# Four of eighteen modulation parts computed by VectorE passes over the weight chunks instead of TensorE matmuls

## The reference, cut to what matters

```python
mx = jnp.split((jax.nn.silu(c) @ w_mod[l] + b_mod[l])[:, None, :], N_MOD, axis=-1)
mz = jnp.split(jax.nn.silu(c_ctx) @ w_mod[l] + b_mod[l], N_MOD, axis=-1)
x = x + 0.5 * mx[2] * swiglu(modulate(rms_norm(x), mx[0], mx[1]), ffn1_w1[l], ffn1_w3[l], ffn1_w2[l])
z = z + 0.5 * mz[2] * swiglu(modulate(rms_norm(z), mz[0], mz[1]), ffn1_w1[l], ffn1_w3[l], ffn1_w2[l])
hx = modulate(rms_norm(x), mx[3], mx[4]) @ w_in[l]
hz = modulate(rms_norm(z), mz[3], mz[4]) @ w_in[l]
...
```

## Time and profile before

| what | value |
|---|---|
| median of 3 runs | 3135.41 us (3133.4 to 3138.79) |
| the profiled execution, its own time | 3135.46 us |
| its span, first to last instruction | 3133.7 us |
| mean granted TensorE clock | 0.989 of 2.4 GHz |
| loads of `w_mod` | 72 of 1 MB |

### The profile page before, as it was taken

The page is one execution under the profiler, slowest core; times in us unless marked ns, Lnnn a source line. Parts: engine busy times, 40 slices in busy tenths (PEclk is TensorE's granted clock), DMA queues, the critical chain, the costliest instruction groups (busy, mean ns, idle before and its releaser), DMA issues.

```text
span 3133.7 us, 54005 instructions
## 1 busy us (share of the span) xinstructions
PE 3013.5 (96%) x23072; PEld 2751.5 (88%) x23072; DVE 1799.8 (57%) x2813; ACT 1480.5 (47%) x2222; POOL 151.3 (5%) x147
## 2 busy tenths in 40 slices
PE   6999999999999998999999989999999999999998
PEld 5899888898889998899898789999899989989997
DVE  4456555656556545455655555465856656486665
ACT  3344454453555443444454444456654445655443
POOL 0000000002000000000200000001010101111000
PEclk9999999999999999999999999999999999999999
DMA  7765445654555555765355445554355655435563
GB/s 276 276 221 167 161 138 199 208 188 144 157 201 174 181 189 202 259 216 168 118 186 169 152 158 188 188 176 129 111 166 190 199 186 163 126 107 170 166 200 133
DMA packets 409691, 556.65 MB, mean 178 GB/s; under 512 B 25277, under 2 KB 357997, under 8 KB 409069
## 3 DMA queue, kind: packets, MB, share of 16 engines
q1 hardware_dynamic: 409452, 553.20, 52.9%
HBM read 552.12 MB, written 1.05 MB: 177 GB/s over the span
## 4 chain that ended last, share of the span: by engine, by line
PE 83%; DVE 8%; DMA 3%; ACT 3%; issue 3%; SPq 0%; POOL 0%; DVEq 0%; ACTq 0%
PE psum L119 24%; PE psum L121 23%; PE psum L120 23%; PE psum L710 1%; DVE wl L276 1%; DMA wr<-in_ffn_w_dram 1%; DVE wl L2166 1%; PE psum L1906 1%; PE psum L2331 1%; PE psum L1528 1%; PE psum L2437 1%; PE psum L2415 1%; PE psum L1183 1%; PE psum L1515 1%; DMA wr<-in_w_mod_dram 1%
## 5 line engine op out<-in xcount | busy, mean ns | idle before, releaser
L276 DVE TENSOR_TENSOR wl<-wr,wh 128x1024 fp32r<-128x1024 f32 (+1 forms) x558 | 658.0, 1215 | 232.2 <-ACT wh L265 231.3
L265 ACT ACTIVATE wh<-wr 128x1024 fp32r<-128x1024 f32 (+1 forms) x558 | 554.5, 1039 | 249.2 <-DMA wr<-in_ffn_w_dram 228.3
L119 PE MATMUL psum<-xt_hi,wh 128*128 128x256 f32 (+1 forms) x2000 | 565.9, 283 | 3.7 <-DVE wl L276 2.4
L120 PE MATMUL psum<-xt_lo,wh 128*128 128x256 f32 (+1 forms) x2000 | 558.1, 279 | 0.0
L121 PE MATMUL psum<-xt_hi,wl 128*128 128x256 f32 (+1 forms) x2000 | 558.0, 279 | 0.0
L2166 DVE TENSOR_TENSOR wl<-wr,wh 128x1024 fp32r<-128x1024 f32 (+3 forms) x336 | 391.8, 1201 | 120.8 <-ACT wh L2158 119.5
L119 PEld LDWEIGHTS psum<-xt_hi,wh 128*128 128x128 f32 (+1 forms) x2000 | 377.3, 189 | 16.0 <-issue 8.1
L120 PEld LDWEIGHTS psum<-xt_lo,wh 128*128 128x128 f32 (+1 forms) x2000 | 376.8, 188 | 2.4
L121 PEld LDWEIGHTS psum<-xt_hi,wl 128*128 128x128 f32 (+1 forms) x2000 | 377.6, 189 | 0.1
L119 PE MATMUL psum<-wh,xt_hi 128*128 128x256 f32 (+1 forms) x1280 | 370.4, 289 | 2.4 <-ACT vv L3316 1.9
L2158 ACT ACTIVATE wh<-wr 128x1024 fp32r<-128x1024 f32 (+3 forms) x336 | 322.5, 997 | 100.8 <-DMA wr<-in_mlp_w_dram 72.2
(11 more groups left out here) (466 smaller groups left out, 5378.9 us busy)
## 6 DMA issues: line engine op xcount, KB each, us to landing
wr<-in_ffn_w_dram SPq DMA_DIRECT2D x231, 1024.0 KB, 5.2
wr<-in_w_in_dram SPq DMA_DIRECT2D x88, 1024.0 KB, 5.1
wr<-in_w_mod_dram SPq DMA_DIRECT2D x72, 1024.0 KB, 4.8
wr<-in_mlp_w_dram SPq DMA_DIRECT2D x64, 1024.0 KB, 5.2
wr<-in_w_out_dram SPq DMA_DIRECT2D x20, 1024.0 KB, 4.9
wr<-in_mem_w_kv_dram SPq DMA_DIRECT2D x8, 1024.0 KB, 4.9
wr<-in_w_branch_dram SPq DMA_DIRECT2D x16, 512.0 KB, 3.4
wr<-in_w_branch_dram SPq DMA_DIRECT2D x8, 1024.0 KB, 4.8
```

Source lines behind the costliest of these rows:

```text
L119: pe.matmul(out, a[0], b[0], start=first, stop=False)
L120: pe.matmul(out, a[0], b[1], start=False, stop=False)
L265: act.activation(self.high[s][:, r], self.raw[s][:, r], ACT.Copy).then_inc(self.highs.sem, 1)
L276: dve.tensor_tensor(self.low[s][:, r], self.raw[s][:, r], self.high[s][:, r].bitcast(F32), ALU.subtract).then_inc(self.lows.sem, 1)
```

## The change

Parts 3 and 4 of layer 0 and parts 4 and 5 of layer 1 (16 of 72 modulation pieces) become `ScaledPiece`s. For each of the 8 blocks of 128 rows of `w_mod` in a part VectorE multiplies the chunk's half [128 x 1024] by a column of one stream and adds it to an accumulator [128 x 1024] for that stream, and the same for the other: four passes for each piece. These passes (`ahead`) stand in VectorE's program in the piece before the scaled one, after its own subtraction steps and ahead of `lo_ahead`. TensorE does nothing in pieces i = 0, 1, 2; in piece 3 it does 16 matmuls with an accumulator block [128 x 128] as weights and one column of ones, which sum over the partitions, and VectorE copies and biases the 16 columns. Pieces 0 to 2 aren't counted as `used` by themselves: the next piece of TensorE waits for the accumulator and adds them to its own increment at its end (`w.use`). In `zf1`, `weave(..., 1, 2)` becomes `weave(..., 1, 3)`, so that its ten modulation pieces stand three pieces apart.

```diff
+    def use(self, last, own=1):
+        last.then_inc(self.used.sem, own + len(self.scaled_by))
+        self.scaled_by = []
...
     def split(self, pe, m):
+        self.scaled(pe)
         pe.wait_ge(self.lows.sem, 2 * self.pieces[m].parted_before + 2)
...
         if not self.over_raw(m + 1):
             self.lo(dve, m + 1, h)
+        if m + 1 < len(self.pieces):
+            self.pieces[m + 1].ahead(dve, h)
...
+class ScaledPiece(ModulationPiece):
+    def wait_scaled(self, eng):
+        mod = self.mod
+        eng.wait_ge(mod.acc.sem, mod.acc.at(2 * self.nth + 2))
+
+    def ahead(self, dve, h):
+        w, b, mod = self.w, self.mod.b, self.mod
+        s = self.m % RING
+        if h == 0:
+            dve.wait_ge(w.loaded[s].sem, w.loaded[s].at(self.m // RING + 1))
...
+        col = 2 * (2 * self.i + h)
+        chunk = w.raw[s][:, :].rearrange("p (k n) -> p k n", n=D)[:, h, :]
+        for v in range(2):
+            acc, scalar = b["acc"][mod.l][:, v, :], b["silu"][:, col + v:col + v + 1]
+            if self.i == 0 and h == 0:
+                last = dve.tensor_scalar(acc, chunk, scalar, None, ALU.mult)
+            else:
+                last = dve.scalar_tensor_tensor(out=acc, in0=chunk, scalar=scalar, in1=acc, op0=ALU.mult, op1=ALU.add)
+        last.then_inc(mod.acc.sem, 1)
+        dve.wait_ge(mod.acc.sem, mod.acc.at(2 * self.nth + h + 1))
+
+    def pe(self, pe, step):
...
+        w.scaled_by.append(self)
+        if self.i == 3:
+            w.scaled(pe)
+            b["ones_set"](pe)
+            bank = w.claim(pe, self.u0)
+            w.touch()
+            for k in range(KT):
+                for v in range(2):
+                    at = 2 * k + v
+                    last = pe.matmul(bank[:, at:at + 1], b["acc"][mod.l][:, v, k * P:(k + 1) * P], b["ones"][:, 0:1], start=True, stop=True)
+            w.use(last, 0)
...
+    def dve(self, dve, step):
...
+        if self.i == 3:
+            w.used_up(dve, self.m)
+            turned = b["turned"][:, 0, 0:2 * KT]
+            dve.tensor_copy(turned, w.ps[:, 6 + self.u0 % 2, 0:2 * KT]).then_inc(w.bank_free[self.u0 % 2].sem, 1)
+            w.emptied(dve, self.u0)
...
-    order += weave(zf1.pieces, M0[10:20], 1, 2)
+    order += weave(zf1.pieces, M0[10:20], 1, 3)
```

More of the change, by code:

```diff
@@ L292, in lo_ahead, with scaled @@
             self.lo(dve, m + 2, 1)
+    def scaled(self, pe):
+        for piece in self.scaled_by:
+            piece.wait_scaled(pe)
+    def use(self, last, own=1):
+        last.then_inc(self.used.sem, own + len(self.scaled_by))
+        self.scaled_by = []
     def split(self, pe, m):
+        self.scaled(pe)
         pe.wait_ge(self.lows.sem, 2 * self.pieces[m].parted_before + 2)
@@ L360, in sp @@
         self.w.load(sp, self.m + RING)
+    def ahead(self, dve, h):
+        pass
     def early(self, eng_name, eng):
@@ L601, in pe @@
                     last = split_product(pe, out[:, t, :], a, b, k == 0, k == self.nk - 1)
-            last.then_inc(w.used.sem if i == self.n_units - 1 else proj.part.sem, 1)
+            if i == self.n_units - 1:
+                w.use(last)
+            else:
+                last.then_inc(proj.part.sem, 1)
     def empty(self, eng, i):
@@ L656, in pe @@
             last = split_product(pe, bank[0:32, 0:256], [v[:, k, :] for v in wv], [v[:, k, :] for v in self.lhs], k == 0, k == KT - 1)
-        last.then_inc(w.used.sem, 1)
+        w.use(last)
     def late(self, name, eng):
@@ L670, in __init__ @@
         self.w, self.l, self.b = w, l, b
-        self.pieces = [ModulationPiece(self, part, i, chunk_of(w_mod, 2 * i * P, 2, part * D, D)) for part in range(9) for i in range(4)]
+        kind = lambda part: ScaledPiece if part in b["scaled"][l] else ModulationPiece
+        self.pieces = [kind(part)(self, part, i, chunk_of(w_mod, 2 * i * P, 2, part * D, D)) for part in range(9) for i in range(4)]
+        self.acc = None
         self.summed = w.share("mod_summed", 36)
@@ L742, in dve, with __init__, ahead @@
         ins.then_inc(mod.summed.sem, 1)
+        w.lo_ahead(dve, self.m)
+class ScaledPiece(ModulationPiece):
+    room = None
+    def __init__(self, mod, part, i, src):
+        super().__init__(mod, part, i, src)
+        self.n_units = 1 if i == 3 else 0
+        self.nth = 4 * sorted(mod.b["scaled"][mod.l]).index(part) + i
+    def wait_scaled(self, eng):
+        mod = self.mod
+        eng.wait_ge(mod.acc.sem, mod.acc.at(2 * self.nth + 2))
+    def ahead(self, dve, h):
+        w, b, mod = self.w, self.mod.b, self.mod
+        s = self.m % RING
+        if h == 0:
+            dve.wait_ge(w.loaded[s].sem, w.loaded[s].at(self.m // RING + 1))
+            if self.i == 0:
+                b["ready"](dve)
+                if self.room:
+                    self.room(dve)
+        col = 2 * (2 * self.i + h)
[4 more added lines that the diff above has]
+                last = dve.tensor_scalar(acc, chunk, scalar, None, ALU.mult)
+            else:
+                last = dve.scalar_tensor_tensor(out=acc, in0=chunk, scalar=scalar, in1=acc, op0=ALU.mult, op1=ALU.add)
+        last.then_inc(mod.acc.sem, 1)
+        dve.wait_ge(mod.acc.sem, mod.acc.at(2 * self.nth + h + 1))
+    def pe(self, pe, step):
+        w, b, mod = self.w, self.mod.b, self.mod
+        self.some(step, 0)
+        w.scaled_by.append(self)
[9 more added lines that the diff above has]
+            w.use(last, 0)
+        self.some(step, 1)
+    def dve(self, dve, step):
+        w, b, mod = self.w, self.mod.b, self.mod
+        w.lo_next(dve, self.m, 0)
+        w.lo_next(dve, self.m, 1)
+        self.some(step, 0)
+        self.some(step, 1)
+        if self.i == 3:
[3 more added lines that the diff above has]
+            w.emptied(dve, self.u0)
+            bias = b["bias"][:, mod.l, self.part * KT:(self.part + 1) * KT].unsqueeze(2).to_broadcast([P, KT, 2])
+            dve.scalar_tensor_tensor(out=b["mod"][mod.l][:, self.part * KT:(self.part + 1) * KT, :],
+                                     in0=turned.rearrange("p (k v) -> p k v", v=2), scalar=0.5 if self.part in (2, 8) else 1.0, in1=bias,
+                                     op0=ALU.add if self.part in (1, 4, 7) else ALU.mult, op1=ALU.add).then_inc(mod.summed.sem, 4)
@@ L3670, in first_block @@
     silu = at("silu_cond", [P, 48], F32, 187)
-    mod_b = dict(mod=c["mod"], silu=silu, turned=mod_turned, bias=c["bias"])
+    mod_ones = small("mod_ones", 1)
+    mod_b = dict(mod=c["mod"], silu=silu, turned=mod_turned, bias=c["bias"],
+                 acc=[at(f"mod_acc{l}", [P, 2, D], F32, (116, 132)[l]) for l in range(LAYERS)], ones=mod_ones, scaled={0: (3, 4), 1: (4, 5)}, ones_set=lambda eng: eng.wait_ge(zeroed.sem, zeroed.at(1)))
     turn_b = dict(tmp=at("affine", [P, 4, 256], F32, 108), diag=c["diag"], var=c["var"], root=c["root"], root_tmp=c["root_tmp"])
@@ L3879, in first_block @@
     urgent, background, order = [], [], []
+    for mod in mods:
+        n = 4 * len(mod_b["scaled"][mod.l])
+        mod.acc = w.share("cond_cleared", 2 * n)
     zf1, xf1 = ffn(0, 1, Z), ffn(0, 1, X)
@@ L3983, in first_block @@
     zf3.down[7].spread(mods[1], 5, X.v, rows2, x_out.wait_added)
+    mods[1].pieces[16].room = xm.turn.wait_done
     x_in1 = InProjection(w, A["w_in"][1], X.pair, X.h, gate_t(X, 1), x_t8.wait_done)
@@ L4107, in gpsimd @@
         w.pool_link = Chain(pool, w.pool_step)
+        pool.memset(mod_ones[:, :], 1.0)
         pool.memset(gw[:, :], 0.0).then_inc(zeroed.sem, 1)
```

## The result

The changed kernel takes 3152.46 us (median of 6 runs, 3147.47 to 3154.46), the kernel before 3134.88 (6 runs, 3132.28 to 3138.79): a ratio of 1.0051, 95% interval 1.0041 to 1.0061, so 17.6 us slower. The profiled execution took 3153.94 (span 3152.2, mean granted clock 0.987), 18.5 more than the one of before, 3135.46.

A forecast was written before the change was run, and what follows sets the result against it. The prediction took TensorE, busy 96% of the span, as the bound. It summed -16.0 + 13.6 + 10.4 + 5.1 = +13.1 onto 3135.4 us, forecasting 3148 us, with a range of 3132 to 3161.

The forecast's parts named there:

- What is taken away: On TensorE, 16 modulation pieces of 1.00 us each go: -16.0 us.
- The 16 one-column matmuls of piece 3: On TensorE, 16 matmuls in each of four parts, at 0.2125 us each, 3.4 us a part: +13.6 us.
- The floor for few columns: Skill page's floor of about 25 ns for 1 to 64 columns: 0.8 us a part, 3.2 in all; not adopted.
- that rival: In piece 3, one-column matmuls are cheap, 0.0625 us a record, +8.0 us: about 3139 us in all; chance 0.12.
- The late load: Next modulation chunk is requested only after the following TensorE piece; eight TensorE waits of 1.3 us: +10.4 us.
- Path 1: On VectorE, late chunk's landing, four passes and the subtraction end at 17.89 us, against a deadline of 16.67.
- path 2: The following piece's own load queues behind the late chunk; its subtraction ends at 17.95 us, against a deadline of 16.67.
- queued loads don't slow the first: On SP's queue, a load requested shortly behind another leaves the first's landing time at 4.8 us.
- The clock: TensorE falls to 1.2 GHz at three of 12 places, 1.7 us each: +5.1 us.
- nothing waits for the gate product: In layer 0, the gate product queued behind the late subtraction lands in time, so no wait comes from it.
- the waits weren't hidden: Rival: late chunk and subtraction are ready by the deadline behind pieces 1 and 2, giving 3133 us; chance 0.11.
- the clock fell at 4 places and not at ten: Rival: TensorE's clock drops at ten to twelve places, 17 to 20 us, giving 3160 to 3164 us; chance 0.12.

The follow-up runs named there:

- experiment 8: Changed kernel with a 32-column selector as weights for the sums, and scaled pieces' buffers released once VectorE's passes are done: 3125.84 us, ratio 0.9965 to the kernel before.
- experiment 3: Changed kernel with 32 equal columns of ones streamed in each of the 16 matmuls instead of one: 3152.17 us, ratio 1.0051 to the kernel before.
- experiment 7: Changed kernel with the sum made by a 32-column selector as weights, accumulators streamed in four column groups: 3138.41 us, ratio 1.0011 to the kernel before.
- experiment 2: Changed kernel with only 2 of the 16 one-column matmuls of a part made, result incomplete: 3141.82 us, ratio 1.0019 to the kernel before.
- experiment 4: Changed kernel with VectorE's first-stream passes left out but the very first, two a piece instead of four: 3153.38 us, ratio 1.0062 to the kernel before.
- experiment 9: Changed kernel with the 32-column selector sum and half of VectorE's passes, first stream's modulation left out: 3132.13 us, ratio 0.9981 to the kernel before.
- experiment 1: Changed kernel with scaled pieces 0 to 2 giving their buffer back once VectorE's passes are done: 3144.88 us, ratio 1.0032 to the kernel before.

## Why the prediction was right or wrong

**What is taken away**, -16.0: right, if a little short. A piece that went gave back 1.1 us. With cheap sums and no late load the four parts are a gain (experiment 8).

**The 16 one-column matmuls of piece 3**, 3.4 us a part: measured 3.49, so 14.0 for 13.6. The row it was taken from, with 64 columns and the same weights, was the right neighbour: 32 columns in place of one changed nothing either (experiment 3). 3.49 / 32 = 0.109 us a record of 128 columns of weights, with the sum of experiment 7 at 1.00 / 16 = 0.0625 for 32 columns of weights and 256 streamed in four groups. The Trainium skill, "TensorE: Matmul & The Clock Gate", section LDWEIGHTS, gives the time of a weight load as its columns divided by 1.2, in ns: an estimate of 0.107 us a record, with which this pace of 0.109 agrees. The floor for few columns that the Trainium skill gives on the same page, section Back-to-back issue gap, and that the prediction had weighed, leaves the weight loads out. By the pace measured that rival is out.

**The late load**, 8 waits of 1.3, +10.4: measured 7 of 1.33 to 1.97, 10.3 in all. Path 1 came out step for step: landing 4.78 for 4.8, passes 5.00 for 5.04, subtraction 2.36, and B' 17.95 behind B where path 1 gave 17.89. i = 0 had no wait, and i = 3 was covered by the matmuls, as experiment 2 showed by uncovering it. Two things were off. One place was hidden by the spread of the columns (line 952), work that stood in the timeline of before and that I hadn't laid against the places. And path 2 was not the equal of path 1: ScalarE began 7.85 after the first request, not 8.81. By that it would have ended 1.0 earlier, and with it deciding (experiment 4) the wait was 0.66 in place of 1.47. That the total agrees to 0.1 us is in part luck: seven waits and not eight, and one of the seven was 0.6 longer than the forecast. The prediction's remark that queued loads don't slow the first can't be read from its, where the first is in use 6.74 us after its request (9.59 - 2.85). The changed kernel bears it out at 11 of 12 places, with landings of 4.75 to 5.02, and not at the twelfth, with 6.25.

**The clock**, 3 drops of 12 places, +5.1: four drops, +6.8. Three stand behind sums, as expected for two. None stands behind the waits of 1.3. The fourth is behind the wait for `gated_lo`, which the prediction didn't list; TensorE was busy for 0.73 of the 3.00 us that end with it. So the price was near, and the places were partly others. Over the kernels with 32 records, 14 of 18 sums were followed by half rate; over those with a short sum (experiments 2, 7, 8 and 9) none of 16 was.

**The step left out**: the wait for `gated_lo` at one place in layer 0 grew from 1.37 to 2.27 us, where the prediction had written that nothing waits for the gate product. VectorE's subtraction ahead of it waited 5.49 for ScalarE, and ScalarE 7.10 for a chunk; that chunk was asked for at 131.14, behind the late pair, and ScalarE began on it 11.6 later (before, 10.3). How much of this is the late load's isn't shown: with the early release the wait was still 2.02 (experiment 1) and 1.62 (experiment 8). Under 1 us by itself.

**The sum**: +13.1 predicted, +17.6 measured, +16.0 by the terms of the trace. Of the 4.5 us between, 1.7 is the clock, 0.9 `gated_lo`, 0.4 the sums, less 0.1 for the waits, and the last 1.6 lies outside these terms. By TensorE's timelines the two stages account for 14.4 of the 17.6. The profiled executions differ by 4 us in untouched code, and runs of the changed kernel lie 7 us apart with mean granted clocks of 0.984 to 0.989; whether the change has a part in that stays open.

**The rivals**: the waits weren't hidden, the small matmuls weren't cheap, and the clock fell at 4 places and not at ten.

## What to carry to other kernels

Work that is taken from the bounding engine also takes its signals along: ask what that engine's count released, and let the engine that now does the work release it. When a sum over partitions has to go through TensorE, make the small operand the weights and stream the large one; the price was that of the weights loaded, 3.49 us against 1.00 for the same sum. Where two paths to a deadline come out equal on paper, each will hide a gain on the other.

## What the runs showed of the hardware

- At the full clock a float32 matmul with 128 x 128 weights takes two records of 0.109 us, whether it streams 1 or 32 columns.
- Stretches of these matmuls fill TensorE's busy time (3.49 of 3.49 us) and yet were followed by 3.4 us or more at 1.2 GHz in 14 of 18 cases. With 32 columns streamed it was two of four.
- Behind the wait for `gated_lo` in layer 0 the half rate followed in six kernels, with waits of 2.02 to 3.29 us, and not in experiment 9, where the wait was the longest, 3.47.
- With the early release and the long sums (experiment 1) the half rate of the profiled execution lasted up to 6.8 us at a time, and took back most of what the waits had given: 3150.2 for this execution, 3138.2 to 3148.5 for the others.
- In the changed kernel a second 1 MB load, asked for 0.4 us behind a first, was in use 7.77 to 8.35 us after the first request at 11 of 12 places, and 9.27 at one; the first landed after 4.75 to 5.02, and 6.25 at that one.
